# Normalizing over the convolution channels: tiles added on VectorE, two products per moment, and other steps for it

## The reference, cut to what matters

```python
def conformer_conv(u, w_dw, b_dw, ln_g, ln_b, w_proj):
    a, gate = jnp.split(u, 2, axis=-1)
    h = a * jax.nn.sigmoid(gate)
    h = lax.conv_general_dilated(h, w_dw, ..., feature_group_count=CONV_CH) + b_dw   # width 31, each channel alone
    h = jax.nn.silu(layer_norm(h, ln_g, ln_b))        # mean and variance over the 1024 channels
    return h @ w_proj

conv_out = conformer_conv(conv_u, ...)
attn_out = windowed_gqa(q, k, v, attn_sink, slopes) @ w_attn_proj    # window 128, a learned sink per head
mixed = (g_conv * conv_out + g_attn * attn_out) @ w_out
x = layer_norm(DEEPNORM_ALPHA * x + mixed, ln1_g, ln1_b)
```

## Time and profile before

| | |
|---|---|
| Median of three runs | 541.55 us (541.47 to 543.19) |
| The profiled execution's own time | 545.22 us |
| Its span | 543.5 us |
| Mean granted TensorE clock | 0.956 |
| TensorE busy | 491.7 us, 90% of the span |
| VectorE busy | 229.9 us, 42% |
| ScalarE busy | 191.6 us, 35% |
| GpSimd busy | 205.0 us, 38% |
| DMA | 145.08 MB, mean 267 GB/s |

### The profile page before, as it was taken

The page is one execution under the profiler, slowest core; times in us unless marked ns, Lnnn a source line. Parts: engine busy times, 40 slices in busy tenths (PEclk is TensorE's granted clock), DMA queues, the critical chain, the costliest instruction groups (busy, mean ns, idle before and its releaser), DMA issues.

```text
span 543.5 us, 7953 instructions
## 1 busy us (share of the span) xinstructions
PE 491.7 (90%) x2882; PEld 347.0 (64%) x2882; DVE 229.9 (42%) x513; ACT 191.6 (35%) x410; POOL 205.0 (38%) x179
## 2 busy tenths in 40 slices
PE   5999999988999998999558989999999999999981
PEld 4999999988999996987455354433334333343430
DVE  2088995797664125530744132222222212222116
ACT  3544455678755366453313121111111111111111
POOL 3897998457568852897000011111111000111000
PEclk9999999998999997999559999999999999999996
DMA  8689975424334531459803877999999999999802
GB/s 295 232 346 359 330 248 170 140 85 155 119 137 155 175 128 42 143 188 385 355 0 97 299 301 290 422 424 420 420 423 422 423 421 421 422 421 421 365 0 78
DMA packets 26367, 145.08 MB, mean 267 GB/s; under 512 B 3040, under 2 KB 3296, under 8 KB 13792
## 3 DMA queue, kind: packets, MB, share of 16 engines
q1 hardware_dynamic: 26336, 144.66, 68.7%
HBM read 143.60 MB, written 1.05 MB: 266 GB/s over the span
## 4 chain that ended last, share of the span: by engine, by line
PE 82%; DVE 8%; ACT 4%; DMA 3%; issue 2%; POOL 1%; ACTq 0%; SPq 0%; DVEq 0%
PE bank L1260 21%; PE bank L1042 11%; PE bank L1279 11%; PE bank L1044 11%; PE bank L1043 11%; PE bank L1292 3%; DMA raw<-in_w_in 3%; PE bank L1293 3%; PE bank L1064 2%; PE bank L1235 2%; PE bank L1190 1%; DVE bank L680 1%; PE bank L1109 1%; ACT kT L601 1%; DVE small L734 1%
## 5 line engine op out<-in xcount | busy, mean ns | idle before, releaser
L402 POOL TENSOR_TENSOR w_lo<-raw,w_hi 128x512 fp32r<-128x512 f32 x140 | 181.6, 1313 | 69.3 <-ACT w_hi L452 65.7
L1042 PE MATMUL bank<-x_hi,w_hi 128*128 128x256 f32 x432 | 127.7, 296 | 5.8 <-POOL w_lo L402 3.5
L1044 PE MATMUL bank<-x_hi,w_lo 128*128 128x256 f32 x432 | 124.0, 287 | 0.0
L1043 PE MATMUL bank<-x_lo,w_hi 128*128 128x256 f32 x432 | 123.9, 287 | 0.0
L452 ACT CAST w_hi<-raw 128x512 fp32r<-128x512 f32 x140 | 85.4, 620 | 88.8 <-PE bank L1044 80.1
L1260 PE MATMUL bank<-slots,raw 128*64 128x512 f32 x496 | 113.4, 595 | 0.0
L419 POOL COPY raw<-gates 128x512 f32 x28 | 19.8, 709 | 205.2 <-PE bank L1260 149.9
L680 DVE SCALAR_TENSOR_TENSOR bank<-slots,par,bank 128x256 f32<-128x256 f32 x232 | 92.7, 484 | 0.1
L1042 PEld LDWEIGHTS bank<-x_hi,w_hi 128*128 128x128 f32 x432 | 84.5, 196 | 8.5 <-issue 5.4
L1043 PEld LDWEIGHTS bank<-x_lo,w_hi 128*128 128x128 f32 x432 | 84.6, 196 | 0.3
L1044 PEld LDWEIGHTS bank<-x_hi,w_lo 128*128 128x128 f32 x432 | 84.6, 196 | 0.0
(11 more groups left out here) (182 smaller groups left out, 536.3 us busy)
## 6 DMA issues: line engine op xcount, KB each, us to landing
slots<-in_w_gate_up SPq DMA_DIRECT2D x62, 1024.0 KB, 12.4
slots<-in_w_down SPq DMA_DIRECT2D x32, 1024.0 KB, 14.0
raw<-in_w_in SPq DMA_DIRECT2D x48, 512.0 KB, 3.7
raw<-in_w_attn SPq DMA_DIRECT2D x8, 512.0 KB, 3.3
raw<-in_w_conv SPq DMA_DIRECT2D x8, 512.0 KB, 3.3
raw<-in_w_out SPq DMA_DIRECT2D x8, 512.0 KB, 3.4
spare<-in_w_gate_up SPq DMA_DIRECT2D x2, 1024.0 KB, 12.7
gates<-in_xT SPq DMA_DIRECT2D x2, 512.0 KB, 5.3
```

Source lines behind the costliest of these rows:

```text
L402: nc.gpsimd.tensor_tensor(w_lo[:, n % SPLIT, m], raw[:, b % RAW, m], w_hi[:, n % SPLIT, m].bitcast(F32), ALU.subtract).then_inc(w_lo_done, 1)
L1042: mm(dst, ah, bh, start=first, stop=False, **kw)
L1043: mm(dst, ah, bl, start=False, stop=False, **kw)
L1044: return mm(dst, al, bh, start=False, stop=last, **kw)
```

## The change

The norm is made in other steps and with fewer products. VectorE adds the finished tile pairs as the taps end (`sum_tiles`), so the mean takes two products (`average`) after block 44. VectorE centres at step 46, ScalarE squares at step 48, VectorE adds the squares (`sum_squares`), and the mean square takes two products after block 48. The root and the table loads stand at ScalarE's step 51, reciprocal and scaling (by tile pairs) at VectorE's step 51, Silu at ScalarE's steps 53 to 55 (three, three and two tiles, each applied twice: once into `x_hi`, once into `acc`, in place of Silu and cast), and the subtractions for `x_lo` at VectorE's step 55. The moments lie in bank 4, the running sums in banks 4 and 3. The taps are spread anew by `taps_in`: none in the score steps 30 to 33, more elsewhere, all done at step 44.

```diff
-TAPS_PER_BLOCK = 6
+def taps_in(b):
+    if b < 20:
+        return 6 + (b + 1) % 2
+    if b < 30:
+        return 7
+    if b < 34:
+        return 0
+    return 4 if b == 34 else 10 if b < 39 else 8
+
+B_MEAN, B_VAR = 44, B_ATTN
+B_SILU = 53
...
@@ ScalarE
+            def conv_silu(tiles):
+                act.wait_ge(x_lo_done, 2)
+                act.wait_ge(block_done, N_IN)
+                for i in tiles:
+                    act.wait_ge(scaled, i // 2 + 1)
+                    g, c = par[:, A_LNG + i:A_LNG + i + 1], par[:, A_LNB + i:A_LNB + i + 1]
+                    nc.scalar.activation(x_hi[:, i, :], acc[:, i, :], ACT.Silu, scale=g, bias=c)
+                    nc.scalar.activation(acc[:, i, :], acc[:, i, :], ACT.Silu, scale=g, bias=c).then_inc(silu_done, 1)
...
+                if b == B_VAR:
+                    for m in range(0, KT, 2):
+                        act.wait_ge(centered, m // 2 + 1)
+                        nc.scalar.activation(square[:, m:m + 2, :], acc[:, m:m + 2, :],
+                                             ACT.Square).then_inc(squared, 1)
+                if b == B_VAR + 3:
+                    act.wait_ge(var_done, 1)
+                    act.wait_ge(consts_set, 4)
+                    nc.scalar.activation(sig[:, 0, :], var_bank, ACT.Sqrt, bias=eps[:, 0:1]).then_inc(std_done, 1)
+                    nc.scalar.activation(mv[:, 0, 3:4], eps[:, 0:1], ACT.Silu)
+                if B_SILU <= b < B_SILU + 3:
+                    conv_silu(range(3 * (b - B_SILU), min(3 * (b - B_SILU) + 3, KT)))
...
@@ VectorE
+            def sum_tiles():
+                while tiles_in[0] < KT and done[0] >= CONV_WIDTH * (tiles_in[0] + 2):
+                    m = tiles_in[0]
+                    tiles_in[0] += 2
+                    if m == 0:
+                        continue
+                    dve.wait_ge(taps_done, CONV_WIDTH * (m + 2))
+                    so_far = acc[:, 0:2, :] if m == 2 else total_bank
+                    if m == KT - 2:
+                        nc.vector.tensor_tensor(sig[:], so_far, acc[:, m:m + 2, :], ALU.add).then_inc(summed, 1)
+                    else:
+                        chained(nc.vector.tensor_tensor(total_bank, so_far, acc[:, m:m + 2, :], ALU.add))
...
+            def sum_squares():
+                for m in range(2, KT, 2):
+                    dve.wait_ge(squared, m // 2 + 1)
+                    so_far = square[:, 0:2, :] if m == 2 else square_bank
+                    if m == KT - 2:
+                        nc.vector.tensor_tensor(sig[:], so_far, square[:, m:m + 2, :],
+                                                ALU.add).then_inc(squares_summed, 1)
+                    else:
+                        chained(nc.vector.tensor_tensor(square_bank, so_far, square[:, m:m + 2, :], ALU.add))
...
+            def scale():
+                dve.wait_ge(std_done, 1)
+                chained(nc.vector.reciprocal(rstd_bank[:, 0:SEQ], sig[:, 0, :]))
+                for m in range(0, KT, 2):
+                    nc.vector.tensor_tensor(acc[:, m:m + 2, :], acc[:, m:m + 2, :],
+                                            rstd_bank[:, 0:SEQ].unsqueeze(1).broadcast_to([P, 2, SEQ]),
+                                            ALU.mult).then_inc(scaled, 1)
...
-                if b < B_CONV:
-                    some_taps(TAPS_PER_BLOCK, (b - 5) // 2 + 1 if b >= 5 else 0)
+                if b <= B_MEAN:
+                    some_taps(taps_in(b) if b < B_MEAN else DVE_TAPS, (b - 5) // 2 + 1 if b >= 5 else 0)
+                    sum_tiles()
+                if b == B_MEAN + 2:
+                    center()
+                if b == B_VAR:
+                    sum_squares()
+                if b == B_VAR + 3:
+                    scale()
+                if b == B_SILU + 2:
+                    for i in range(KT):
+                        dve.wait_ge(silu_done, i + 1)
+                        nc.vector.tensor_tensor(x_lo[:, i, :], acc[:, i, :], x_hi[:, i, :].bitcast(F32),
+                                                ALU.subtract).then_inc(c_lo_done, 1)
...
@@ TensorE
+            def average(dst, done):
+                for a in range(2):
+                    ins = mm(dst, mean_ones[:], sig[:, a, :], start=(a == 0), stop=(a == 1))
+                ins.then_inc(done, 1)
...
+                if b == B_MEAN:
+                    pe.wait_ge(summed, 1)
+                    average(mean_bank, mean_done)
+            for b in range(B_ATTN, B_CONV):
                 column_block(b, a_hi, a_lo, o_lo_done if b == B_ATTN else None)
+                if b == B_VAR:
+                    pe.wait_ge(squares_summed, 1)
+                    average(var_bank, var_done)
+            pe.wait_ge(std_done, 1)
             pe.wait_ge(s_xt, 16)
             pe.wait_ge(alpha_set, 1)
             residual(first=True)
```

More of the change, by code:

```diff
@@ L43 @@
 N_BLOCKS = N_IN + 3 * KT
-VAR_PAIR = B_CONV // 2
 Q_BLOCK, V_BLOCK, GATE_BLOCK = 16, 28, 32
@@ L208, in encoder_kernel @@
         tap_bank, rstd_bank = bank[3], bank[7]
-        var_bank = pair_bank[VAR_PAIR % PSUM_PAIRS]
+        mean_bank, var_bank, total_bank = bank[4][:, 0:SEQ], bank[4][:, SEQ:2 * SEQ], bank[4][:].rearrange(
+            "p (a t) -> p a t", a=2)
+        square_bank = bank[3][:].rearrange("p (a t) -> p a t", a=2)
         out_bank = [bank[3], bank[4], bank[5], bank[6]]
@@ L240, in encoder_kernel @@
         mean_done, centered, squared, var_done = (sem(n) for n in ("mean_done", "centered", "squared", "var_done"))
-        std_done, scaled, silu_done, c_hi_done, c_lo_done = (
-            sem(n) for n in ("std_done", "scaled", "silu_done", "c_hi_done", "c_lo_done"))
+        summed, squares_summed = sem("summed"), sem("squares_summed")
+        std_done, scaled, silu_done, c_lo_done = (sem(n) for n in ("std_done", "scaled", "silu_done", "c_lo_done"))
         dve_step = sem("dve_step")
@@ L510, in _ @@
             for b in range(N_BLOCKS):
[L511 to L536, removed]
+                if b not in NATIVE:
                     split_hi(b)
@@ L696, in some_taps, with center @@
                     done[0] += 1
+            tiles_in = [0]
+            def sum_tiles():
[10 more added lines that the diff above has]
+                        chained(nc.vector.tensor_tensor(total_bank, so_far, acc[:, m:m + 2, :], ALU.add))
+            def center():
+                dve.wait_ge(mean_done, 1)
+                for m in range(0, KT, 2):
+                    nc.vector.tensor_tensor(acc[:, m:m + 2, :], acc[:, m:m + 2, :],
+                                            mean_bank.unsqueeze(1).broadcast_to([P, 2, SEQ]),
+                                            ALU.subtract).then_inc(centered, 1)
+            def sum_squares():
[10 more added lines that the diff above has]
+                chained(nc.vector.reciprocal(rstd_bank[:, 0:SEQ], sig[:, 0, :]))
+                for m in range(0, KT, 2):
+                    nc.vector.tensor_tensor(acc[:, m:m + 2, :], acc[:, m:m + 2, :],
+                                            rstd_bank[:, 0:SEQ].unsqueeze(1).broadcast_to([P, 2, SEQ]),
+                                            ALU.mult).then_inc(scaled, 1)
             def evacuate(q):
@@ L801, in _ @@
             for b in range(N_BLOCKS):
[L802 to L813, removed]
-                        nc.vector.tensor_tensor(acc[:, i, :], acc[:, i, :], rstd_bank[:, 0:SEQ],
-                                                ALU.mult).then_inc(scaled, 1)
-                    for i in range(KT):
-                        dve.wait_ge(c_hi_done, i + 1)
-                        nc.vector.tensor_tensor(x_lo[:, i, :], acc[:, i, :], x_hi[:, i, :].bitcast(F32),
-                                                ALU.subtract).then_inc(c_lo_done, 1)
                 if b == 2:
```

19 lines of the change are left out of this document (removed).

## The result

The changed kernel takes 533.58 us (median of four, 531.77 to 536.62), the kernel before 542.37 beside it: ratio 0.984, interval 0.980 to 0.987. Five more executions on another occasion gave 533.80 against 542.55 (0.983, interval 0.981 to 0.986). That is 8.8 us, where 11.8 to 12.0 were forecast; the time lies inside the stated range, near its upper end, and outside the 527.5 to 531.5 us that the forecast gave its own case (A). The profiled execution took 536.62 us, with a span of 534.9 and a clock of 0.959.

What follows compares the result with a forecast made beforehand. TensorE, 82% of the chain of waits, was taken as the bound; -5.2 - 5.8 + 1.2 - 2.0 = -11.8 us gave 529.7 from the median 541.55, 529.5 with a clock share; range 526.5 to 534.5.

Steps and rivals of the forecast that it cites:

- rival A: Whole kernel: the forecast's own case, 529.5 us, range 527.5 to 531.5; chance 0.58.
- rival C: Blocks 52 to 55: ScalarE and GpSimd starve TensorE, idle 3 not 1.2, one more low-clock stretch, 533 to 535 us; chance 0.14.
- Moments: After blocks 44 and 48: sixteen plain-f32 products become four, 12 x 0.433 = 5.2 us off TensorE's path.
- the cover: At both moments: VectorE's sums end before TensorE asks, about 2 us for the mean, at worst 0.4 for the squares.
- New idle under the projection: Before blocks 52 and 55: TensorE waits 0.36 and 0.85 us for weights, 1.2 us new idle, bounds 0.4 to 3.
- Blocks 56 and 57: First convolution blocks: 3.7 us lost there goes, 3.4 of it low clock; with the 2.13 us idle before, 5.8.
- Taps: Score steps, blocks 30 to 33: without taps the last maximum and block 36 come 2.0 us earlier.
- B: Block 36: no fall of the clock there, 1.5 us less, 528.0 us; chance 0.17.
- D: After block 44: TensorE waits for VectorE's sum as taps fall behind, 536 us, 538 with low clock; chance 0.06.
- E: Blocks 49 to 57: short idles keep TensorE at 1.2 GHz, slower than before, 558 us at worst; chance 0.03.
- F: Score steps: they give nothing because something else holds block 36, 531.5 us; chance 0.02.

Runs made afterwards that it cites:

- e3: Changed kernel with eight products for each moment again, at the new places and behind the same waits: 537.25 us, ratio 0.990.
- e4: Changed kernel with Silu on two tiles in each of steps 52 to 55, not three, three and two in 53 to 55: 533.41 us, ratio 0.986.
- e11: Kernel before, with four unread products between the residual and block 56 to fill TensorE's idle: 542.05 us, ratio 1.000.
- e1: Kernel before with only the new spread of the taps, none in the score steps; norm as before: 540.99 us, ratio 0.997.
- e2: Changed kernel with six taps in each score step again and 24 fewer in steps 35 to 43: 535.72 us, ratio 0.986.
- e5: Changed kernel with the maxima of the scores written to PSUM, not SBUF: 535.09 us, ratio 0.984.
- e12: Changed kernel with four unread products between blocks 35 and 36 to fill TensorE's idle: 534.13 us, ratio 0.982.
- e9: Changed kernel with e5, e7 and e4 together: 533.01 us, ratio 0.981.
- e7: Changed kernel with ScalarE's cast of block 36 ahead of the copies of v and the first normalization: 530.66 us, ratio 0.979.
- e10: Changed kernel with the edits of e9 and unread products that keep TensorE busy in the router: 525.34 us, ratio 0.966.
- the repairs: The edits of e5, e7 and e4 made together in the changed kernel: 533.01 us, ratio 0.981.

## Why the prediction was right, and where it was off

**The range.** The measured 533.58 us lies within 526.5 to 534.5, but not within the 527.5 to 531.5 of rival A, the forecast's own case. It lies where rival C was priced (533 to 535), and C's mechanism did not come: 0.95 us of idle in blocks 52 to 55, and no low clock after it. So the steps below were largely right, and that the time fell into the range is in part luck: the room left for C took up two errors of another kind, the low clock counted at blocks 56 and 57 and the last maximum.

**Moments.** -5.2, measured 5.20 (e3). Right, and so was the cover: VectorE was 2.2 us ahead of TensorE for the mean (forecast 2) and 1.6 for the squares (forecast at least 0.4). The sums took 1.67, 0.68 and 0.69, and 0.85, 0.70 and 0.69 us, within 0.02 of the values taken or less.

**New idle under the projection.** +1.2 forecast as 0.36 and 0.85; measured 0.23 and 0.72, 0.95 in all, both released by GpSimd. Right, and e4 shows that ScalarE's queue holds the second. The rule on two SBUF inputs was weighed at the right place: the eight `x_lo` took 6.05 us, five of them 0.42 as in the earlier trace rows and the last three 1.51, by turns with GpSimd, whose five subtractions took 7.06. One of those was on the way to block 55, as the prediction allowed for: it stands from 193.15 to 194.69, 0.26 longer than the 1.28 of one alone, and block 55 starts at 194.75. Block 56 wasn't made late:

```profile
L890 DVE TENSOR_TENSOR x_lo<-slots,x_hi x8: 417/418/1514, 191.8 to 196.3; 128x256 fp32r<-128x256 f32 x8
...
193.15 7.06 POOL L417 TENSOR_TENSOR w_lo<-raw,w_hi 128x512 fp32r<-128x512 f32 x5 [1.44 <-ACT w_hi L467]
```

One reading under that rule was off. The 0.69 us of line 720 were not taken alone: VectorE began at 229.99, between two subtractions, and the one that begins at 230.04 took 1.80 us. There GpSimd waited for VectorE, which fits the rule as well.

**Blocks 56 and 57.** This is the step that failed most: "so 3.7 us, of which 6.83/2 = 3.4 is the low clock and the rest waits between tiles". Against its own profile it was right. As a statement on the kernel it was not: e11 and e1 show that at full clock TensorE loses 1.88 us there to the tiles alone, 0.2 more with 3.41 us of low clock, and 1.8 more with 6.83. The profiled execution of before was one with much low clock: with the falls of 3.41 and 6.83 its clock was 0.956, the lowest value there is: 7 of the 45 later executions of that kernel have it, and their median is 0.963. The prediction then subtracted the whole sum from the median too ("I subtract the same from it"), and so counted low clock as a gain that the median execution didn't have, as far as its clock tells. Worth about 1.8 us.

**Taps.** -2.0 forecast, 1.24 measured (e1, e2). The walk took the last maximum at 2.37 us behind its scores, much as the first one, which "came at 100.80, 2.2 us after its scores". It overlooked that the handing over of the maximum has two SBUF inputs, so the rule that the same text applied to `x_lo` holds for it. The Trainium skill (SBUF — State Buffer, "SBUF: two separate sides") has that such an instruction and one of GpSimd that reads SBUF shut each other out for the whole instruction, and names no size. The runs agree: 128x4 elements took 0.92 us until GpSimd was done, and 0.16 with one input in PSUM (e5). In the kernel before it took 0.43 at that place and ended with GpSimd's subtraction too (116.77 and 116.76); moved earlier by the change, it met more of that instruction. 0.76 us.

**The sum.** Like for like, without falls, the table gives for before 160.06 + 1.23 - 0.2 = 161.1 between the marks (e1, with the 1.23 of its taps put back and the 0.2 of its fall taken off) and for the changed kernel 151.85: 9.24 us. The idles have to be counted from start to start for this, since the idle time in a row leaves out how much the products around it are spread. In a full stream a product starts every 0.12 us. Before block 55 of the second profile the last one starts at 191.82, the next at 192.82 and the one after it at 193.04, which is 0.98 more, where the row says 0.72; at block 52 it is 0.47 for 0.23. From the residual's start to the second product of block 56 are 5.92 us in before and 3.56 in the changed kernel, 2.36 for the 2.13. With these the parts give 5.20 + 1.24 + 2.36 + 1.88 - 1.45 = 9.23, and nothing is left over. The forecast's 11.8 less 1.8 for the clock, 0.76 for the maximum, and 0.25 the other way for the idles comes to 9.5; the rest is that way of counting. The medians say 8.8, within what the draw of the clock allows.

**Rivals.** B (no fall at block 36) came true in some executions and not in others, with 1.49 us between them (153.34 and 151.85), as priced. C, D, E and F did not happen, though the time is one that C was given.

**What stays open.** Between the two profiles of the changed kernel lie 2.3 us from the transposes to the end (284.2 and 281.9). The stretch at 0.50 at the start of the experts makes 1.36 of them (5.01 and 3.65 for the 16 products above). Another 1.06 are there before: in both, the router's stretch at 0.50 is 27.3 us long, but it ends 28.4 us after the first transpose in one and 26.0 in the other, and the first product of the experts starts at 29.28 and 28.22. (The 0.06 too much come back later.)

What brings the stretch at the experts isn't shown. It stood in five of the twelve profiles without the added products in the router (the first of the changed kernel, e2, e5, e12, e9), and not in before, the second of the changed kernel, e1, e3, e4, e7 and e11. In three of the five a fall after block 36 stood too, but not in e9 and e12, so it isn't its consequence. It goes with the place of the router's stretch: that ended 28.3 to 29.0 us after the first transpose in the five, and 26.0 to 27.9 in the seven. No run moves that place alone, so this is what twelve profiles have in common and not a cause that is shown. e7 had none and a steady 530.0 to 530.9, e9 did less work in the same stretch and was slower. Whether e7's order is better or five executions were lucky isn't settled by these runs.

## What to carry to other kernels

A profile is one draw: before a low-clock stretch goes into a sum, see whether the profiled execution's clock is that of the median, and compare variants between marks in the trace, with the falls of the clock written beside them. Work on a critical engine that is counted in equal instructions (16 products to 4) is worth what it says, 5.20 for 5.2, even where that engine idles later on, if what it idles for follows its own progress. A tiny VectorE instruction with two SBUF inputs on a critical chain can wait for most of a GpSimd instruction (0.92 us where it takes 0.16); one operand in PSUM took that away. And where TensorE must idle at another engine's pace, work that nobody reads can pay: 5.8 us here by medians.

## What the runs showed of the hardware

- The clock fell after an idle of 1.9 us in some executions and not in others of the same kernel, with the same idle (1.89 and 1.90). The fall after block 36 stood in five of ten profiles with that idle, and in none of four without it (e7, e9, e10, e12). With the 2.13 us before block 56 mostly filled (e11), no fall followed there in the one profile; the two profiles with all of that idle had one, of 6.83 and of 3.41 us.
- In the router, where TensorE is busy 13.07 of 22.82 us, the clock is at 0.50 for a stretch of 27.3 us. With twelve more products it stands at 0.83, and with the repairs at 1.00, though the products there are the same.
- Low clock and waits overlap: 3.41 us at 0.50 cost 1.49 where TensorE had its operands (after block 36), 0.2 where they came one by one (block 56), and 1.36 at the start of the experts.
- A VectorE instruction of 128x4 elements with two SBUF inputs ended within 0.02 us of a GpSimd subtraction in three of four cases and took up to 0.92 us. With one input in PSUM it took 0.16 four times of four (e5).
